# Moving ScalarE's rounding of weight chunks to the end of a step, and VectorE's rests from three chunks ahead to two

## The chip, the cores and the metric

The kernel runs on one core of one Trainium2 chip. Its time is the device time of one execution in microseconds (us). The core has a matrix engine (TensorE, PE in the rows), a vector engine (VectorE, DVE), a scalar engine (ScalarE, ACT), GpSimd (POOL) and a queue engine (SyncE, SP). Each engine works through its own program in order, and semaphores tie the five programs together. SP, POOL and ACT also issue DMA transfers between HBM and the on-chip memory.

## The reference

One inference step of one layer of a hybrid decoder, in float32. The 512 prompt positions and the 8 decode sequences (one new token each) go through the same weights, so the kernel handles 520 columns at once. What matters here, cut short:

```python
xn = rms_norm(x, norm1_g)
proj = xn @ w_in                    # D_MODEL 2048 -> pool 512, conv 3*512, q/k/v 3*1024, 8 forget logits
y_pool, y_conv = causal_pool_mix(...), h_b * causal_dwconv(h_c * h_x, prev_conv, conv_w)
q, k = rms_norm(q, q_norm_g), rms_norm(k, k_norm_g)     # 8 heads of 128
y_att = attn_fn(q, k, v, logf)      # prompt: causal, 512 x 512 per head
                                    # decode: 8 sequences, each over 4096 cached positions (32 pages of 128)
mix = concat([rms_norm(y_pool), rms_norm(y_conv), rms_norm(y_att)])
x = x + mix @ w_o
a, gate = split(rms_norm(x, norm2_g) @ w_up)            # 2048 -> 2 * 5632
x = x + (silu(causal_dwconv(a) + b) * gate) @ w_down    # 5632 -> 2048
```

The cached keys and values of the decode sequences are 256 pages each, and a page is 128 positions by 1024 numbers (512 KB).

## The kernel before

**Products in three parts.** A float32 product is made of three products of rounded numbers: a number is a rounded head plus a rest (`xh` and `xl` for the activations, `wh` and `wl` or `wlr` for the weights), and PE adds head times head, head times rest and rest times head. ScalarE makes the head of the weights (a Copy from the raw weights `wraw` to `wh`, in `head`), VectorE the rest (`wraw` minus `wh`, in `tile_rest` in the first part of the program, to `wlr`).

**Tiles, chunks and steps.** The input projection has 40 tiles of 128 output columns. A tile's weights are two *chunks* of 8 blocks of 128 x 128, so chunks 2t and 2t+1 belong to tile t, and there are `CHUNKS` = 80. The program of every engine is written as a loop over steps s. In PE's step s (2 to 79) stands `half_tile(s // 2, s % 2)`: the even step does the first 260 of tile s/2's columns, the odd one the other 260. So PE needs chunk 2t at the start of step 2t and chunk 2t+1 in the middle of step 2t. `half_tile` waits for `w_lo`, which counts the rests. The chunks are released (`w_used`) in the odd step, at its middle and at its end. `wh` has four slots, so the head of chunk c may be made once chunk c-4 is released. `wlr` has room for eight chunks.

**Raw weights.** `wraw` has two slots of 2 MB, each with four chunks. SP issues the load for chunks 4n to 4n+3 at the end of its step 4n-5, behind that step's key pages, and waits there until PE has finished its own step 4n-5 (line 683; `w_used`).

**What ScalarE does in a step.** In an odd step s it makes the head of chunk s+3, moves PE's accumulator of the half tile away (`keep_half`, with the 8 decode columns into `projS`), and makes the head of chunk s+4. In an even step it only moves the accumulator. After these come the stages of the pool mixer and of the prompt's attention heads (`pool_out`, `prompt_head`), and after all of it, where a sequence's value sum is complete, the move of that sum to `osb` (the `V_LAST` part).

**What VectorE does in a step.** Softmax bookkeeping of the decode sequences, stages of the prompt heads, then one page of keys times the query (`key_page`, line 1857: eight instruction pairs, one for each head), then `tile_rest(s + 3)`, then mixer parts, then the step's other two or three key pages. Key pages come through a ring of four buffers. SP issues the load of a page when VectorE has used the page four before it. All key pages (SP) and raw weights (SP) stand in one queue.

**Value pages.** PE multiplies them inside `half_tile` (two at a time), and POOL loads them into a second ring of four.

After step 79 come the mixers' norms, the output projection with the remaining value pages, and the feed-forward part, which is the longer half of the run.

Of the kernel before, what the change touches and what calls it, by code (L numbers as in the profile page):

```python
# [49 lines left out]
CHUNKS = 80  # L50
# [98 lines left out]
def hybrid_layer_kernel(nc, a, o):  # L149
    ctx = ExitStack()  # L150
    with ctx:
# [271 lines left out]
        def square_place(n):  # L423
            return stg[:, 0, 0:SEQ] if n < 14 else sq_late
# [842 lines left out]
        def _(act):  # L1267
            seq = Count(act_seq)

            def copy(out, in_):  # L1270
                return act.activation(out, in_, ACT.Copy)  # L1271
# [62 lines left out]
            def raw_chunk(c, down):  # L1334

                raw, q = wraw[:, (c // 4) % 2, :], c % 4
                if down:
                    return raw.rearrange("p (k n) -> p k n", k=FG)[:, :, q * 256:(q + 1) * 256]
                m, half = divmod(q, 2)
                return raw.rearrange("p (k n) -> p k n", k=KT)[:, half * 8:half * 8 + 8, m * P:(m + 1) * P]  # L1340

            def blocks(buf, c, down):
                return buf[:, c % 4, :].rearrange("p (k n) -> p k n", k=FG if down else 8)

            def head(g, c, down=False):

                if c % 4 == 0:
                    n = g // 4 + c // 4
                    late = 0 if n <= R_F else (n % 2) + 1
                    act.wait_ge(w_loaded[n % 2], 16 * (n // 2 + 1 + late))  # L1350
                act.wait_ge(w_used, g + (c + 1))
                copy(blocks(wh, c, down), raw_chunk(c, down)).then_inc(w_hi, 1)
# [39 lines left out]
            def keep_half(t, b):  # L1392

                place = tile_place(t)
                if b == 0:
                    place_free(t)
                    act.wait_ge(half_full, t + 1)
                    copy(place[:, 0:HALF], ps[:, 0, 0:HALF]).then_inc(acc_free[0], 1)
                    return
                act.wait_ge(w_used, 4 + 2 * t + 2)  # L1400
                copy(place[:, HALF:SEQ], ps[:, 1, 0:SEQ - HALF])
                copy(projS[:, TILES[t]:TILES[t] + 1, :], ps[:, 1:2, SEQ - HALF:HALF]).then_inc(acc_free[1], 1)
                act.wait_ge(acc_free[1], t + 2)
                act.sem_inc(tile_kept, 1)
# [24 lines left out]
            def mix_square(n, y):  # L1429
                act.wait_ge(x_sum, n)  # L1430
                act.activation(square_place(n), y, ACT.Square).then_inc(x_sq, 1)

            def mix_rstd(n, bank, size, place):

                act.wait_ge(x_tot, n)
                act.activation(place, ps[:, bank, :], ACT.Ln, bias=epsc[:, :], scale=1.0 / size).then_inc(x_log, 1)
                act.wait_ge(x_log, n)
                act.activation(place, place, ACT.Exp, scale=-0.5).then_inc(x_rb, 1)
# [82 lines left out]
            for s in range(SLOTS):  # L1521
# [11 lines left out]
                if s < CHUNKS and s % 2 == 0:  # L1533
                    keep_half(s // 2, 0)
                if s < CHUNKS and s % 2:
                    head(0, s + 3)
                    keep_half(s // 2, 1)
                    head(0, s + 4)
                if s == 8:
                    act.wait_ge(p_tr, 1)  # L1540
                    copy(stT, ps[:, 2, 0:480].rearrange("p (g b) -> p g b", g=POOL_G)).then_inc(p_stT, 1)
# [31 lines left out]
                if s == CHUNKS:  # L1573
                    mix_rstd(2, 2, 1024, msum[2])
                    for g in (2, 3):
                        act.wait_ge(v_done, g + 1)
                        mix_square(12 + g, ymix[:, 4 + g, 0:SEQ])
                if s == CHUNKS + 1:
                    mix_rstd(3, 5, 512, msum[1])
                    act.wait_ge(r_full, 2)  # L1580
                    copy(rows_s[64:64 + 2 * CONV_T, :], ps[64:64 + 2 * CONV_T, 3, 0:P]).then_inc(r_copied, 1)
                    copy(rows_s[32:32 + CONV_T * DEC, :], ps[32:32 + CONV_T * DEC, 3, P:2 * P]).then_inc(r_copied, 1)
# [99 lines left out]
        def _(dve):  # L1682
            seq = Count(dve_seq)

            def tt(out, in0, in1, op):
                return dve.tensor_tensor(out, in0, in1, op)  # L1686
# [64 lines left out]
            def raw_chunk(c, down):  # L1751
                raw, q = wraw[:, (c // 4) % 2, :], c % 4
                if down:
                    return raw.rearrange("p (k n) -> p k n", k=FG)[:, :, q * 256:(q + 1) * 256]
                m, half = divmod(q, 2)
                return raw.rearrange("p (k n) -> p k n", k=KT)[:, half * 8:half * 8 + 8, m * P:(m + 1) * P]
# [4 lines left out]
            def tile_rest(c):  # L1761

                dve.wait_ge(w_hi, c + 1)
                m, half = divmod(c % 4, 2)
                kept = wlr[:, (c // 4) % 2, :].rearrange("p (k n) -> p k n", k=KT)[:, half * 8:half * 8 + 8, m * P:(m + 1) * P]
                tt(kept, raw_chunk(c, False), blocks(wh, c, False).bitcast(F32), ALU.subtract).then_inc(w_lo, 1)
# [328 lines left out]
            for s in range(SLOTS):  # L2095
                softmax(s)
                if s == 6:
                    page_sums()
                if s == 8:
                    page_biases()  # L2100
                if s == 14:
                    value_lanes()
                if s == 9:
                    pool_rows()
                if s in (OWN_Q, OWN_Q + 5):
                    own_q((s - OWN_Q) // 5)
                kp = [divmod(n, PAGES) for n in KEYS.get(s, [])]
                at_head = head_stages(s)
                for h, stage in at_head:
                    prompt_head(h, stage)  # L2110
                if s in (OWN_K, OWN_K + 4):
                    sample_keys((s - OWN_K) // 4)
                if kp:
                    key_page(*kp[0])
                if s + 3 >= 4 and s + 3 < CHUNKS:
                    tile_rest(s + 3)
                if pool_slot(s) is not None:
                    pool_part(pool_slot(s))
                if s == POOL0 + 2:
                    dve.wait_ge(e_kept, 4)  # L2120
                    step(dve, seq, dve.memset(sums_pool, 0.0))
                if pool_slot(s - 2) is not None:
                    mix_sum(pool_slot(s - 2))
                for g in range(CONV_T):
                    if g < 2 and s == CONV_AT[g] + 2:
                        mix_sum(4 + g)
                    if s == CONV_AT[g]:
                        conv_part(g)
                if s == 28:
                    dve.wait_ge(d_loaded, 16)  # L2130
                    dve.tensor_scalar(crow, crow, -1.0, None, ALU.mult).then_inc(h_cm, 1)
                    dve.wait_ge(y_stored, 96)
                    dve.memset(msum[2], 0.0)
                if s == CHUNKS - 1:
                    mix_sum(13)
                if s == CHUNKS:
                    mix_sum(14)
                    mix_sum(15)
                if s == CHUNKS + 1:
                    dve.wait_ge(h_O, HEADS)  # L2140
                    dve.wait_ge(h_stored[1], 16 * HEADS)
                    dve.wait_ge(y_stored, 16 * 14)
                    for c in range(4):
                        weight_rest(0, CHUNKS + c)
                    dve.wait_ge(r_stored, 112)
                    sample_squares(0, 8)
                if s == CHUNKS + 2:
                    for t in range(0, 8, 2):
                        mix_pair(t)
                if s == CHUNKS + 3:  # L2150
                    for t in range(8, 16, 2):
                        mix_pair(t)
                if s == OUT0 + 1:
                    sample_sums(0, 2, Y_TOT)
                    sample_scale(0, 2, Y_RS)
                if s == OUT0 + 2:
                    step(dve, seq, dve.memset(sumsq[1], 0.0))
                if s >= OUT0:
                    c = s - OUT0
                    weight_rest(0, CHUNKS + c + 4)  # L2160
                    if c % 2 and c >= 3:
                        out_sum(c // 2 - 1)
                    if c % 2:
                        out_tile(c // 2)
                if s == LAST + 2:
                    sample_mix()
                    sample_squares(8, 16)
                if s == LAST + 3:
                    sample_sums(2, 3, YA_TOT)
                if s == LAST + 4:  # L2170
                    sample_scale(2, 3, YA_RS)
                for n in kp[1:]:
                    key_page(*n)
# [125 lines left out]
```

## Time and profile before

| | |
|---|---|
| median of 3 runs | 2797.38 us (2797.11 to 2801.74) |
| the profiled execution | 2798.29 us, span of the profile 2796.3 us |
| PE busy over the span | 94% |
| the stretch of steps 2 to 79 | about 89 to 905 us |
| PE busy in that stretch | 725.19 of 816 us |
| DMA engines busy in that stretch | 0.93 |

Times in rows are microseconds from the start of the span. A row of the timeline has the start, the length, the engine, the line of the kernel, the operation and its tiles. In brackets stands how long the engine had been idle before it, and who released it. Busy time of PE is modelled for pipelined matmuls, so the gaps in front of its matmuls say more than its share.

### The profile page before, as it was taken

The page shows a single profiled execution, that of the slowest core. Times are in us where ns is not written, and L with a number is a line of the kernel's source. Part 1 is how long each engine was busy: PE and PEld are TensorE (multiplying, and loading weights), DVE is VectorE, ACT ScalarE, POOL GpSimd, SP SyncE. Part 2 cuts the span into 40 slices and gives each one's busy share as a digit, 9 for nine tenths or more (in the row PEclk, how much of TensorE's full clock was granted, in tenths as well). Part 3 has the DMA queues.
Part 4 walks back from the last instruction along what each step waited for, and adds up shares of the span by engine and source line. Part 5 has one row for each costly group of instructions (what it writes and reads, how often), then busy time and mean ns, then how long its engine had stood idle before and what let it go on. Part 6 is the DMA issues. An engine that isn't in the chain of part 4 may idle for free.

```text
span 2796.3 us, 50751 instructions
## 1 busy us (share of the span) xinstructions
PE 2617.2 (94%) x19729; PEld 2342.8 (84%) x19729; DVE 1425.7 (51%) x5631; ACT 735.1 (26%) x1029; POOL 160.9 (6%) x326
## 2 busy tenths in 40 slices
PE   6788789999988799889999999999999999999998
PEld 3676667777776356569999999999999999999998
DVE  5698768767867622244434343434343434343433
ACT  5222123333332311132222222222222222222221
POOL 0100111111111122100000000000000000000000
PEclk8888889999989799979999999999999999999999
DMA  8778999999999897652222222222222222222221
GB/s 297 242 243 299 335 334 364 360 359 359 335 328 363 323 314 265 218 186 84 93 96 91 91 91 91 91 91 91 91 91 91 91 91 91 91 91 91 91 91 65
DMA packets 272292, 524.55 MB, mean 188 GB/s; under 512 B 16148, under 2 KB 181693, under 8 KB 270740
## 3 DMA queue, kind: packets, MB, share of 16 engines
q1 hardware_dynamic: 218717, 365.71, 38.0%
q0 software_dynamic: 39760, 142.46, 13.8%
q10 hardware_dynamic: 13575, 13.14, 1.4%
q8 instruction: 155, 2.54, 0.4%
q14 instruction: 85, 0.70, 0.1%
HBM read 501.84 MB, written 17.76 MB: 186 GB/s over the span
## 4 chain that ended last, share of the span: by engine, by line
PE 70%; DMA 13%; DVE 11%; issue 3%; SPq 2%; ACT 1%; POOL 0%; DVEq 0%; POOLq 0%; ACTq 0%
PE ps L749 69%; DMA t_r<-in_cache_k 9%; DVE t_r L1857 8%; DMA t_r<-in_cache_v 2%; DMA t_wraw<-in_w_in 1%; SPq L630 1%; PE ps L752 1%; DVE t_stg L1742 0%; DVE t_wlr L1686 0%; DVE t_S L1857 0%; DVE t_auxL L1686 0%; DVE t_work L1686 0%; DVE t_xl L1686 0%; SPq L683 0%; ACT t_wh L1271 0%
## 5 line engine op out<-in xcount | busy, mean ns | idle before, releaser
L749 PE MATMUL ps<-t_xh,t_wh 128*128 128x260 f32 (+1 forms) x4352 | 1080.3, 299 | 33.4 <-DVE t_wlr L1686 19.6
L749 PE MATMUL ps<-t_xl,t_wh 128*128 128x260 f32 (+1 forms) x4352 | 1053.1, 294 | 0.0
L749 PEld LDWEIGHTS ps<-t_xh,t_wh 128*128 128x128 f32 x4352 | 745.8, 193 | 166.7 <-issue 119.2
L1686 DVE TENSOR_TENSOR t_wl<-t_wraw,t_wh 128x1024 fp32r<-128x1024 f32 x296 | 362.3, 1225 | 843.7 <-ACT t_wh L1271 843.7
L1271 ACT ACTIVATE t_wh<-t_wraw 128x1024 fp32r<-128x1024 f32 x376 | 398.5, 1060 | 1479.9 <-PE ps L749 1369.8
L749 PEld LDWEIGHTS ps<-t_xl,t_wh 128*128 128x128 f32 x4352 | 744.7, 193 | 10.7 <-issue 1.4
L749 PE MATMUL ps<-t_xh,t_wl 128*128 128x260 f32 (+1 forms) x3072 | 677.1, 294 | 0.0
L1857 DVE CUSTOM_DVE_ANT_0 t_r<-t_r,t_work 128x128 f32<-128x128 f32 x2048 | 455.4, 286 | 175.3 <-DMA t_r<-in_cache_k 159.0
L749 PEld LDWEIGHTS ps<-t_xh,t_wl 128*128 128x128 f32 x3072 | 487.5, 189 | 11.8
L749 PE MATMUL ps<-t_xh,t_wlr 128*128 128x260 f32 x1280 | 376.1, 294 | 0.0
L749 PE MATMUL ps<-t_hh,t_wh 128*128 128x260 f32 x1408 | 282.8, 282 | 3.4 <-issue 3.4
L749 PE MATMUL ps<-t_hl,t_wh 128*128 128x260 f32 x1408 | 284.4, 283 | 0.0
L749 PE MATMUL ps<-t_hh,t_wl 128*128 128x260 f32 x1408 | 284.2, 283 | 0.0
L749 PEld LDWEIGHTS ps<-t_xh,t_wlr 128*128 128x128 f32 x1280 | 257.3, 201 | 0.0
L1686 DVE TENSOR_TENSOR t_r<-ps,t_r 128x520 f32<-128x520 f32 (+1 forms) x184 | 128.5, 699 | 226.8 <-PE ps L749 226.8
L749 PEld LDWEIGHTS ps<-t_hh,t_wh 128*128 128x128 f32 x1408 | 217.1, 189 | 4.5 <-issue 3.7
L749 PEld LDWEIGHTS ps<-t_hh,t_wl 128*128 128x128 f32 x1408 | 216.6, 189 | 0.0
L749 PEld LDWEIGHTS ps<-t_hl,t_wh 128*128 128x128 f32 x1408 | 216.4, 188 | 0.0
L749 PE MATMUL ps<-t_r,t_work 128*8 128x512 f32 x1040 | 163.5, 629 | 33.4 <-DMA t_r<-in_cache_v 23.7
L552 POOL DMA_DIRECT2D t_r<-in_cache_v x256 | 135.7, 530 | 847.4 <-PE ps L749 820.5
L1857 DVE DVE_READ_ACCUMULATOR2_ANT t_S<- 128x1 f32 x2048 | 167.0, 82 | 0.1
L1686 DVE TENSOR_TENSOR t_wlr<-t_wraw,t_wh 128x1024 fp32r<-128x1024 f32 x80 | 97.4, 1219 | 12.1 <-ACT t_wh L1271 12.1
(305 smaller groups left out, 1243.0 us busy)
## 6 DMA issues: line engine op xcount, KB each, us to landing
t_r<-in_cache_k SPq DMA_DIRECT2D x256, 512.0 KB, 6.7
t_r<-in_cache_v POOLq DMA_DIRECT2D x256, 512.0 KB, 7.0
t_wraw<-in_w_up SPq DMA_DIRECT2D x44, 2048.0 KB, 8.0
t_wraw<-in_w_down SPq DMA_DIRECT2D x22, 2048.0 KB, 7.8
t_wraw<-in_w_in SPq DMA_DIRECT2D x21, 2048.0 KB, 16.2
t_wraw<-in_w_o SPq DMA_DIRECT2D x11, 2048.0 KB, 14.0
scr_x<-t_r POOLq DMA_DIRECT2D x1, 4160.0 KB, 20.0
t_work<-in_x_prompt SPq DMA_DIRECT2D x4, 1024.0 KB, 6.6
```

The costliest lines, as they stand in the source:

```text
L552: pool.dma_start(vring[:, n % RING, :], v_pages[bass.ds(g, 1), :, :].rearrange("a p n -> (a p) n")).then_inc(v_loaded[n % RING], 16)
L630: return sp.value_load(ptr[0:1, bass.ds(n, 1)], min_val=0, max_val=N_POOL - 1)
L749: return pe.matmul(out, lhsT, rhs, start=start, stop=stop)
L752: return pe.transpose(out, in_, ident[0:n, 0:n])
L1271: return act.activation(out, in_, ACT.Copy)
L1686: return dve.tensor_tensor(out, in0, in1, op)
L1857: last = dve.tensor_tensor_reduce(out=kring[:, p % RING, h * HD:(h + 1) * HD], in0=kring[:, p % RING, h * HD:(h + 1) * HD], in1=qcur[r % 2 ...
```

## The change

ScalarE's two heads of an odd step are taken out of their places around the accumulator's move. In their stead each step from 1 to 80 makes one head, of chunk s+3, behind the accumulator's move, the pool mixer's parts and the stages of the prompt heads. VectorE's step makes the rest of chunk s+2 instead of s+3, at the same place in the step.

```diff
@@ ScalarE, step s @@
                 if s < CHUNKS and s % 2:
-                    head(0, s + 3)
                     keep_half(s // 2, 1)
-                    head(0, s + 4)
...
                         mix_square(12 + g, ymix[:, 4 + g, 0:SEQ])
+                if 1 <= s <= CHUNKS:
+                    head(0, s + 3)
                 if s == CHUNKS + 1:
@@ VectorE, step s @@
                     key_page(*kp[0])
-                if s + 3 >= 4 and s + 3 < CHUNKS:
-                    tile_rest(s + 3)
+                if 4 <= s + 2 < CHUNKS:
+                    tile_rest(s + 2)
```

The same heads and rests are made, in the same numbers. The programs of PE, SP and POOL are unchanged, row for row.

ScalarE before, from step 28's end to step 30: the head of chunk 32, the two moves of step 29's accumulator (`t_work<-ps`, `t_projS<-ps`), the head of chunk 33, head 0's logarithms and exponential, then the move of the first sequence's value sum (`t_work<-ps 128x512`) and step 30's accumulator.

```order
L1271 ACTIVATE t_wh<-t_wraw 128x1024
L1271 ACTIVATE t_work<-ps 128x252
L1271 ACTIVATE t_projS<-ps 128x8
L1271 ACTIVATE t_wh<-t_wraw 128x1024
L1469 ACT_TABLE_LOAD
L1469 ACTIVATE t_auxL<-ps,t_epsc 128x512
L1470 ACTIVATE t_auxL<-ps,t_epsc 128x512
L1473 ACT_TABLE_LOAD
L1473 ACTIVATE t_auxL<-t_auxL 128x1024
L1271 ACTIVATE t_work<-ps 128x512
L1271 ACTIVATE t_auxL<-ps 128x260
```

And now, the same place: the accumulator's moves of step 29 first, then the head stage, then the head of chunk 32, then the value sum, then step 30's accumulator and behind it the head of chunk 33.

```order
L1271 ACTIVATE t_work<-ps 128x252
L1271 ACTIVATE t_projS<-ps 128x8
L1469 ACT_TABLE_LOAD
L1469 ACTIVATE t_auxL<-ps,t_epsc 128x512
L1470 ACTIVATE t_auxL<-ps,t_epsc 128x512
L1473 ACT_TABLE_LOAD
L1473 ACTIVATE t_auxL<-t_auxL 128x1024
L1271 ACTIVATE t_wh<-t_wraw 128x1024
L1271 ACTIVATE t_work<-ps 128x512
L1271 ACTIVATE t_auxL<-ps 128x260
L1271 ACTIVATE t_wh<-t_wraw 128x1024
```

Chunk 32's head moved from before the accumulator to behind the exponential, and chunk 33's from step 29 to step 30.

VectorE, the first place of difference: its step 1, between the forget gate's instructions and the first key page.

```order
 L1809 SCALAR_TENSOR_TENSOR t_work<-t_work 8x520
 L1810 SCALAR_TENSOR_TENSOR t_work<-t_work 8x512
-L1686 TENSOR_TENSOR t_wlr<-t_wraw,t_wh 128x8x128
 L1857 ISA t_r,t_S<-t_r,t_work 128x128
 L1857 ISA t_S 128x1
```

One rest is gone there and one appears at the end, in step 77. At the 75 places between, the rows read alike, and each now makes the rest of the chunk before the one that it made.

## Rows read from the trace of the kernel before

**Rows 1.** Windows: stretch, its us; busy PE, PEld, DVE, ACT, POOL; PEclk, DMA, GB/s.

```profile
89.00:905.00 816.00, 725.19 (x5079) 596.02 (x5079) 624.89 (x4358) 241.00 (x435) 92.78 (x175) 0.91 0.93 333
400.00:905.00 505.00, 473.61 (x3374) 378.19 (x3372) 375.76 (x2662) 170.75 (x317) 65.31 (x123) 0.95 0.97 354
1254.00:2796.00 1542.00, 1530.48 (x12715) 1528.37 (x12714) 616.57 (x911) 362.61 (x411) 5.08 (x10) 1.00 0.27 90
```

**Rows 2.** Waits from 89 to 905 us: total, times, longest.

```profile
DVE t_r L1857 <- DMA t_r<-in_cache_k: 159.0, 40, 12.2
ACT t_wh L1271 <- DMA t_wraw<-in_w_in: 80.2, 10, 16.5
...
PE ps L749 <- DVE t_auxL L1958: 21.3, 4, 7.5
PE ps L749 <- DVE t_wlr L1686: 19.6, 4, 10.2
...
DVE t_wlr L1686 <- ACT t_wh L1271: 3.8, 2, 2.9
...
PE ps L749 <- ACT t_auxL L1271: 3.4, 1, 3.4
```

**Rows 3.** Timeline of SP: raw weights (L683) and key pages (L634).

```profile
263.20 0.39 SPq L683 DMA_DIRECT2D t_wraw<-in_w_in  x1
265.44 46.67 SPq L634 DMA_DIRECT2D t_r<-in_cache_k  x14
...
397.56 0.39 SPq L683 DMA_DIRECT2D t_wraw<-in_w_in  x1
...
857.16 0.39 SPq L683 DMA_DIRECT2D t_wraw<-in_w_o  x1
```

**Rows 4.** Timeline of VectorE: first key page behind raw weights, and rests.

```profile
283.56 0.29 DVE L1857 CUSTOM_DVE_ANT_0 t_r<-t_r,t_work 128x128 f32<-128x128 f32 x1 [9.29 <-DMA t_r<-in_cache_k]
...
285.27 1.22 DVE L1686 TENSOR_TENSOR t_wlr<-t_wraw,t_wh 128x1024 fp32r<-128x1024 f32 x1
...
291.97 1.22 DVE L1686 TENSOR_TENSOR t_wlr<-t_wraw,t_wh 128x1024 fp32r<-128x1024 f32 x1
...
413.43 0.29 DVE L1857 CUSTOM_DVE_ANT_0 t_r<-t_r,t_work 128x128 f32<-128x128 f32 x1 [11.19 <-DMA t_r<-in_cache_k]
...
425.11 1.21 DVE L1686 TENSOR_TENSOR t_wlr<-t_wraw,t_wh 128x1024 fp32r<-128x1024 f32 x1
```

**Rows 5.** Timeline of PE: its gaps, and the passage from step 29 to 30.

```profile
127.27 0.58 PE L749 MATMUL ps<-t_xh,t_wh 128*128 128x260 f32 x1 [10.15 <-DVE t_wlr L1686]
286.55 0.39 PE L749 MATMUL ps<-t_xh,t_wh 128*128 128x260 f32 x1 [4.45 <-DVE t_wlr L1686]
332.90 0.59 PE L749 MATMUL ps<-t_xh,t_wh 128*128 128x260 f32 x1 [3.94 <-DVE t_wlr L1686]
362.41 1.88 PE L749 MATMUL ps<-t_auxL,t_ones 128*128 128x512 f32 x4
374.15 1.04 PE L749 MATMUL ps<-t_r,t_work 128*8 128x512 f32 x4 [7.70 <-issue]
```

**Rows 6.** Timeline of ScalarE: moves of accumulators and heads of chunks.

```profile
299.75 0.36 ACT L1271 ACTIVATE t_work<-ps 128x252 f32<-128x252 f32 x1
...
366.05 1.06 ACT L1271 ACTIVATE t_wh<-t_wraw 128x1024 fp32r<-128x1024 f32 x1 [9.13 <-DMA t_wraw<-in_w_in]
367.01 0.36 ACT L1271 ACTIVATE t_work<-ps 128x252 f32<-128x252 f32 x1
...
373.47 0.58 ACT L1271 ACTIVATE t_work<-ps 128x512 f32<-128x512 f32 x1
...
432.95 0.38 ACT L1271 ACTIVATE t_work<-ps 128x252 f32<-128x252 f32 x1 [2.97 <-PE ps L749]
```

**Rows 7.** The window behind the gap that ends at 374.15.

```profile
374.00:379.00 5.00, 4.85 (x22) 3.18 (x23) 4.76 (x46) 0.05 (x1) 1.06 (x2) 0.50 0.55 167
```

**Rows 8.** Part 6 of the page: load, KB each, median us from issue to landing.

```profile
t_wraw<-in_w_in SPq DMA_DIRECT2D x21, 2048.0 KB, 16.2
```

## The prediction

> **What bounds the kernel now.** I read the windows first, since the change acts only while the input projection runs, about 89 to 905 us. From 1254 us on PE is busy without a break at the full granted clock (1.00) [rows 1]: that half can't move, and what the change costs or gives before it comes out one for one at the end. In the stretch itself three things are close to full at once: PE 725.19 of 816 us, the DMA engines 0.93, VectorE 624.89 of 816. From 400 us on PE is at 473.61 of 505 and the DMA engines at 0.97 [rows 1]. So nobody has much room, and what counts is which wait joins the three.
>
> The table of waits says which. VectorE waits for key pages (159.0 us in 40 waits) and hardly for ScalarE's heads (3.8). PE waits for VectorE's rests four times, 19.6 us in all, and for an accumulator's move once, 3.4 [rows 2]. ScalarE waits 80.2 us for raw weights [rows 2], in every fourth step ahead of the accumulator's move.
>
> The pattern is one of four steps, since SP loads raw weights every fourth step. Take the group that begins when SP issues raw weights at 263.20, at the end of PE's step 19, and the key page of step 20 behind them at 265.44 [rows 3]. That page is used at 283.56, after VectorE idled 9.29 us for it [rows 4]. The 2048 KB of raw weights go ahead of it in the queue, and take 16.2 us to land in the median [rows 8]. Right behind the page stands the rest of chunk 23 (285.27, done 286.49), and PE, which stood in the middle of step 22, starts again at 286.55 after 4.45 us of idleness [rows 5]. The waits at 127.27 and 332.90 are the same wait, for chunks 7 and 27. So already the lead of three chunks runs out once every four steps, for the odd chunk whose rest stands behind the late key page.
>
> **The change part by part.**
>
> *Rests one step later.* No rest is added: 76 of 1.22 us stay in the stretch. But the rest of a chunk now stands where that of the next one stood. For chunk 23 this is the place at 291.97, done at 293.19 [rows 4], 6.7 us later than 286.49, at a point where PE waits already. I put every chunk's new place (the next rest's end before) against the time at which PE reached it. Of the 75 chunks 4 to 78, 35 would come late, the worst of each group of four from chunk 4 to 67 by 13, 4, 3, 0, 8, 10, 9, 8, 3, 5, 8, 4, 8, 3, 1 and 1 us, and from step 68 on none.
>
> *What a late rest costs.* If VectorE went on undisturbed, PE would fall behind once, by the worst lateness, 8 to 13 us, and then have its rests in time. It would win back what it now idles for VectorE. But VectorE isn't undisturbed: SP issues the raw weights only when PE has finished the fourth step, and the key pages queue behind them. That closes a loop: end of PE's step 4m+3, raw weights and key page, VectorE's step 4m+4, in step 4m+5 the rest of chunk 4m+7, PE from the middle of step 4m+6 to the end of 4m+7. Its length from the first group: 20.4 us (263.20 to 283.56) plus 9.6 (to 293.19) plus 13.2 (286.55 to the move at 299.75 [rows 6]) = 43.2 us, where that group took 36.6 (263.20 to 299.75). In the group from 397.56: 15.9 to 413.43, 12.9 to 426.32, 13.2 = 42.0, where it took 35.4 (to 432.95). So the loop adds 6.6 us to each of these two. The 14 groups between 263.20 and 857.16 [rows 3] take 42.4 us on average: the long ones (47 to 50 us) hide the loop, the short ones don't. Lining up all 19 groups by this sum, each with its own three parts, nine are lengthened: by 5.3, 5.8, 0.9, 7.9, 4.7, 3.7, 2.7, 7.7 and 0.8, 39 us in all. That is the upper bound.
>
> *What comes off it.* First, the page behind the raw weights comes sooner when PE, not VectorE, is last to release them, since the earlier key pages have then landed: 15.9 us in the group from 397.56, against 20.4 and an average of 17.7. I take 2 us off in each of 8 groups, 16 us. Second, PE's gaps that VectorE or ScalarE cause go when PE is later: 21.3 us in four waits for the pool mixer (they swallow the 5.3 of the first group), 7.70 at 374.15. Of these I take 14. 
>
> *Heads behind the stages.* ScalarE is busy 241.00 of 816 us, and a head is 1.06 us. Chunk 23's head now comes after step 20's accumulator instead of after step 19's. VectorE takes it in step 21, behind 291: 20 us later. So heads cost nothing; the cover is VectorE's lag of over a step, and if that went, each head would hold VectorE up by a few us. The gain is that the move and the head stages no longer stand behind the wait for raw weights. It shows once on the path: at 366.05 the head of chunk 32 ended a wait of 9.13 us, behind it came step 29's accumulator at 367.01, the head stage, and at 373.47 the value sum's move, for which PE waited 7.70 us, to 374.15 [rows 5, 6]. Now the stage, 4.9 us of work in front of that move, begins behind step 29's end (362.41, where PE sums the head's squares [rows 5]) and passes during that wait; a head of 1.06 stands behind it, and the sum moves at about 370, 3 to 4 us sooner. This is in the 14 above.
>
> Sum: 39 - 16 - 14 + 4 = +13 us. The profiled execution took 2798.29, within 1 us of the median 2797.38. **Forecast 2810 us.**
>
> *A rule against the trace.* The trace has 20.4 us for a key page behind raw weights, while value pages share the engines. The Trainium skill (DMA: Bandwidth & Descriptors, Queues, rings and completion order) says that each DMA engine goes round-robin over the queues that have work. By it a stalled PE, which frees no value pages, would hand its share to SP's queue. No run here separates the two queues. What it would make of the time is rival B.
>
> **The rivals.**
>
> A, *all is passed on*: the loop binds as computed and nothing is absorbed, +39, 2836 us. For it: the DMA share of 0.97 and PE's 473.61 of 505. Against: VectorE-caused gaps exist and would close. Chance 0.14.
>
> B, *the lateness is absorbed*: while PE stalls, no value pages are asked for, and the key page lands sooner. The raw weights (2048 KB) and one page (512 KB) are 2.6 MB; at 354 GB/s [rows 1] that is 7.4 us instead of 17.7, so the loop would shrink to about 33 us, under any group. Then PE only lags once and takes it back in its other gaps: 2797 to 2802 us. Against: PE's stall comes after the page has landed, not before. Chance 0.13. By the Trainium skill's rule this would be the likelier one.
>
> C, *faster*: the loop's lateness is absorbed as in B and ScalarE's freed moves decide. The gap of 7.70 us goes with its slow clock of 5 us (2.5), and the 3.4 for an accumulator with it, up to 12 us with what the earlier head stages save at the pool mixer: 2786 us. It decides if PE waits for rests less than 20 us in all, as now. For it: 80.2 us of waits for raw weights stand before ScalarE's moves. Against: PE waited for a move of an accumulator just once. Chance 0.15.
>
> **How the numbers follow.** The forecast, slower by 6 to 28 us, has 0.58; A 0.14, B 0.13, C 0.15. A measurement of this kernel can't tell a difference under 0.2% (5.6 us) from none. Slower by more: 0.58 + 0.14 = 0.72; within it B, 0.13; faster C, 0.15. The range from 2789 to 2832 leaves out the outer part of A and of C, about 0.07 each. The forecast's own range is 2803 to 2826.
>
> **What would show it.** In the changed profile PE's waits for `t_wlr` rise from 19.6 us to 50 to 90, ten or more of them, at the start and in the middle of steps 4m+2. VectorE's waits for key pages stay near 159 or rise. SP's raw issues wait more for PE. The last accumulator's move (step 79) comes 8 to 25 us later than before. The wait of 7.70 at 374.15 shrinks, and PE's waits for the pool mixer's `t_auxL` L1958 fall under 21.3. ScalarE's waits for raw weights shift behind the moves; VectorE's for heads stay under 15. I would be wrong if PE's waits for rests stay near 20, or if they rise and step 79 still ends at its old time.

## The result, and the profile after

| | before | after |
|---|---|---|
| median | 2796.86 us, 6 runs (2793.4 to 2801.74) | 2820.47 us, 6 runs (2811.73 to 2828.52) |
| profiled execution | 2798.29 us, span 2796.3 us | 2819.47 us, span 2817.5 us |
| ratio | | 1.0074, 95% interval 1.006 to 1.0089 |

The change makes the kernel slower by 0.74%, which is 20.7 us, where +13 us was forecast. (This goes by the ratio. The two medians of the table lie 23.6 us apart, the two profiled executions 21.2.) The windows of the kernel after have the same columns as [rows 1]:

```profile
89.00:914.70 825.70, 724.93 (x5062) 599.04 (x5062) 621.19 (x4323) 231.62 (x431) 90.66 (x172) 0.91 0.91 325
400.00:928.00 528.00, 481.55 (x3384) 384.13 (x3382) 383.90 (x2680) 170.33 (x321) 65.74 (x124) 0.94 0.95 343
1275.00:2817.00 1542.00, 1530.62 (x12732) 1528.22 (x12731) 617.24 (x912) 363.99 (x412) 5.08 (x10) 1.00 0.27 90
```

The last row is the late half, 1542 us as before, with 1530.62 us of PE against 1530.48. So the whole difference arises in the input projection. The accumulator's last move (step 79) starts at 914.7 us, before at 894.0: 20.7 us later. From 400 us on the DMA engines fell from 0.97 to 0.95 and from 354 to 343 GB/s [rows 1]: the same bytes took longer.

The first row ends at that last move. For the kernel before the same row, cut at its own last move, is:

```profile
89.00:894.00 805.00, 719.78 (x5061) 595.19 (x5061) 616.93 (x4295) 235.91 (x430) 90.26 (x171) 0.91 0.92 332
```

PE was busy 5.15 us longer for the same matmuls. The other 15.4 us of the 20.7 are waits. What PE waited for in that stretch, after the change (total, times, longest):

```profile
PE ps L749 <- DVE t_wlr L1686: 68.5, 23, 7.2
PE ps L749 <- DVE t_auxL L1958: 9.6, 3, 4.6
...
PE ps L749 <- issue: 2.6, 2, 2.3
```

All of PE's waits add up to 103.6 us in ten kinds, before to 88.2 in thirteen. Waits for rests grew from 19.6 us in 4 times [rows 2] to 68.5 in 23, by 48.9. All others together shrank from 68.6 to 35.1, by 33.5: the mixer's from 21.3 to 9.6, those of the kind "issue" (the 7.70 us at 374.15 among them [rows 5]) from 13.1 to 2.6. What ScalarE and VectorE waited for in the kernel after:

```profile
DVE t_r L1857 <- DMA t_r<-in_cache_k: 165.0, 35, 13.1
...
ACT t_wh L1271 <- DMA t_wraw<-in_w_in: 2.6, 2, 2.4
```

ScalarE's wait for raw weights has shrunk from 80.2 us to 2.6, and VectorE's 3.8 us for heads [rows 2] have no row any more. SP's program shows the other side of PE's lateness. Its wait for PE ahead of the raw weights, before:

```profile
SPq L683 <- PE ps L749: 28.4, 7, 9.4
```

and after:

```profile
SPq L683 <- PE ps L749: 61.3, 14, 11.2
```

So in 14 of the 20 loads PE is now last to release SP, before in 7. One turn of the loop, of the group that begins at 399.14. SP issues raw weights, and the next key page behind them:

```profile
399.14 0.39 SPq L683 DMA_DIRECT2D t_wraw<-in_w_in  x1
401.94 1.55 SPq L634 DMA_DIRECT2D t_r<-in_cache_k  x1
```

VectorE idles for the page, makes the rest behind it, and in the next step the other one:

```profile
415.07 0.29 DVE L1857 CUSTOM_DVE_ANT_0 t_r<-t_r,t_work 128x128 f32<-128x128 f32 x1 [12.09 <-DMA t_r<-in_cache_k]
...
416.78 1.22 DVE L1686 TENSOR_TENSOR t_wlr<-t_wraw,t_wh 128x1024 fp32r<-128x1024 f32 x1
...
426.64 1.22 DVE L1686 TENSOR_TENSOR t_wlr<-t_wraw,t_wh 128x1024 fp32r<-128x1024 f32 x1
```

PE starts right behind that rest (done at 427.86):

```profile
427.92 0.59 PE L749 MATMUL ps<-t_xh,t_wh 128*128 128x260 f32 x1 [5.50 <-DVE t_wlr L1686]
```

and the accumulator of step 35 is moved at 441.69, where SP's next load of raw weights is issued, behind a wait for PE. The three parts are 15.9, 12.8 and 13.8 us (399.14 to 415.07, to 427.86, and 427.92 to 441.69), 42.5 in all. The prediction had 15.9, 12.9 and 13.2 for this group. Its other worked group did not come out: from the end of step 19 to that of step 23 it forecast 43.2 us, and the trace has 38.3 (265.9 to 304.2), against 36.5 before. The key page came 17.4 us after the load instead of 20.4, and PE waited once, for the rest right behind that page (5.8 us, to 286.1), and not for the one a step later.

**Where the 20.7 us arise.** The stretch can be cut at the end of step 31, which is 397.8 us before and 399.4 after. The windows before:

```profile
89.00:397.80 308.80, 249.38 (x1697) 216.43 (x1698) 247.00 (x1680) 68.98 (x116) 27.47 (x52) 0.85 0.85 299
397.80:894.00 496.20, 470.39 (x3365) 378.76 (x3363) 369.93 (x2616) 166.93 (x315) 62.79 (x119) 0.95 0.97 353
```

and after:

```profile
89.00:399.40 310.40, 248.65 (x1698) 215.31 (x1699) 249.34 (x1696) 67.38 (x117) 27.96 (x53) 0.88 0.84 297
399.40:914.70 515.30, 476.29 (x3366) 383.73 (x3364) 371.85 (x2627) 164.24 (x315) 62.70 (x119) 0.94 0.95 342
```

| | first part, before | after | second part, before | after |
|---|---|---|---|---|
| length | 308.8 | 310.4 | 496.2 | 515.3 |
| PE's waits for rests | 18.5 | 47.9 | 1.0 | 20.6 |
| PE's other waits | 40.8 | 16.7 | 24.4 | 18.0 |

So 47.9 of the 68.5 us of waits for rests stand in the first part, and they cost 1.6 us there: PE's other waits fell by 24.1. The second part has 20.6 of them and 19.1 of the 20.7 us. In five of its twelve groups of four steps (those behind the ends of steps 31, 39, 43, 51 and 75) SP waited for PE at the raw weights, VectorE for the key page behind them and PE for a rest. These five are 25.2 us longer than before, the other seven 6.1 us shorter in sum. The trace of VectorE's half of the change alone (below) has the same split: 51.8 of its 75.5 us of waits for rests in the first part, which took 312.3 us, and 510.6 us for the second. These are single executions, and six of the kernel after spread over 17 us, so the split is good to some us only.

### The profile page after: what moved, and what is told of

Same layout as the page of the kernel before. It is cut to its first block, busy times and chain, and to the rows that moved or that the text cites. A ratio compares the mean times of both kernels' runs of the same rounds, so it can differ in the third digit from the quotient of the medians.

```text
span 2817.5 us, 50751 instructions
## 1 busy us (share of the span) xinstructions
PE 2621.4 (93%) x19729; PEld 2345.9 (83%) x19729; DVE 1426.2 (51%) x5631; ACT 731.1 (26%) x1029; POOL 160.7 (6%) x326
## 3 DMA queue, kind: packets, MB, share of 16 engines
q0 software_dynamic: 39760, 142.46, 13.8%
## 4 chain that ended last, share of the span: by engine, by line
PE 74%; DMA 11%; DVE 9%; issue 3%; SPq 2%; ACT 1%; POOL 0%; POOLq 0%; DVEq 0%; ACTq 0%
PE ps L749 73%; DMA t_r<-in_cache_k 8%; DVE t_r L1857 6%; DMA t_r<-in_cache_v 3%; DMA t_wraw<-in_w_in 1%; SPq L630 1%; PE ps L752 1%; DVE t_wlr L1686 1%; DVE t_stg L1742 0%; SPq L634 0%; DVE t_auxL L1686 0%; DVE t_xl L1686 0%; SPq L649 0%; DVE t_S L1857 0%; DVE t_work L1686 0%
## 5 line engine op out<-in xcount | busy, mean ns | idle before, releaser
L749 PE MATMUL ps<-t_xh,t_wh 128*128 128x260 f32 (+1 forms) x4352 | 1084.4, 300 | 82.8 <-DVE t_wlr L1686 68.5
L749 PEld LDWEIGHTS ps<-t_xl,t_wh 128*128 128x128 f32 x4352 | 747.4, 194 | 10.6 <-issue 1.2
L1857 DVE DVE_READ_ACCUMULATOR2_ANT t_S<- 128x1 f32 x2048 | 174.4, 85 | 0.1
L1271 ACT ACTIVATE t_work<-ps 128x512 f32<-128x512 f32 (+7 forms) x81 | 38.2, 486 | 287.6 <-PE ps L749 263.1
## 6 DMA issues: line engine op xcount, KB each, us to landing
t_wraw<-in_w_in SPq DMA_DIRECT2D x21, 2048.0 KB, 15.9
```

Source lines behind the costliest of these rows:

```text
L749: return pe.matmul(out, lhsT, rhs, start=start, stop=stop)
L1857: last = dve.tensor_tensor_reduce(out=kring[:, p % RING, h * HD:(h + 1) * HD], in0=kring[:, p % RING, h * HD:(h + 1) * HD], in1=qcur[r % 2 ...
```

## The experiments

Three theories about the +20.7 us stood before the first runs. **L**: a late rest makes PE late, PE makes SP's raw weights late, and with them the key page and the next rests. **H**: ScalarE's new places cost. **O**: PE lags once and the rest is absorbed. Each kernel ran beside the kernel before on one chip; the ratios are to that one. The median of before beside them was 2800.9, 2800.4 and 2801.6 us in the three batches.

### ScalarE's half of the change alone

```diff
-                    head(0, s + 3)
                     keep_half(s // 2, 1)
-                    head(0, s + 4)
...
+                if 1 <= s <= CHUNKS:
+                    head(0, s + 3)
```

> ScalarE as in the changed kernel (heads behind the stages), VectorE as before (rest of chunk s+3). Theory L (the late rests cost the time, through the loop of raw weights and key pages): the rests keep their old places, so the time is near the kernel before, 2795 to 2804 us, with PE's waits for t_wlr at 15 to 30 us. VectorE should now wait for heads for the first time, 10 to 40 us in all in t_wlr <- t_wh, mostly near steps 31, 59, 67, 70 and 71, where it is less than a step behind PE. Rival H (ScalarE's heads or moves in their new places cost the time): 2812 to 2822 us.

Measured: 2803.91 us, ratio 1.0013 (1.0002 to 1.0024). Its waits:

```profile
DVE t_r L1857 <- DMA t_r<-in_cache_k: 116.2, 31, 12.2
DVE t_wlr L1686 <- ACT t_wh L1271: 55.2, 13, 9.1
PE ps L749 <- DVE t_wlr L1686: 22.0, 5, 10.2
```

With the rests left at three chunks ahead, VectorE does run into the later heads: 55.2 us, where before it was 3.8 [rows 2]. It costs little: VectorE waits 42.8 us less for key pages (159.0 to 116.2). H is out as the cause: 0.13% of 0.74%.

### VectorE's half alone

```diff
-                if s + 3 >= 4 and s + 3 < CHUNKS:
-                    tile_rest(s + 3)
+                if 4 <= s + 2 < CHUNKS:
+                    tile_rest(s + 2)
```

> ScalarE as before, VectorE as in the changed kernel (rest of chunk s+2). Theory L: all of the loss is here, 2813 to 2824 us, PE's waits for t_wlr 60 to 75 us; a few us more than the changed kernel if the earlier moves of accumulators and value sums give something (the wait of 7.70 us at step 30 would be there again). Rival H: 2794 to 2801 us.

Measured: 2822.66 us, ratio 1.0074 (1.0046 to 1.0101), the whole loss of the change.

```profile
PE ps L749 <- DVE t_wlr L1686: 75.5, 26, 9.6
```

SP waited 57.7 us for PE in 13 loads, about as in the kernel after. ScalarE's half neither adds nor takes away beside it.

### The change, with rests ahead of the step's first key page

```diff
-                if kp:
-                    key_page(*kp[0])
                 if 4 <= s + 2 < CHUNKS:
                     tile_rest(s + 2)
+                if kp:
+                    key_page(*kp[0])
```

> The changed kernel, but in each step the rest of chunk s+2 stands ahead of the step's first key page, not behind it. The chunk that stood behind the page that comes after the raw weights (4m+6) is then free of it, and the rest of chunk 4m+7 comes about 3 us sooner after that page (one page of 1.9 us and one rest of 1.2 us less in front of it). Theory L: the loop is 3 us shorter in each group, so more than half of the loss is gone: 2800 to 2810 us, PE's waits for t_wlr at 20 to 40 us. Rival O (PE merely lags once behind VectorE and no loop is closed): the one lateness shrinks by 3 us, 2812 to 2819 us.

Measured: 2807.48 us, ratio 1.0021 (1.0008 to 1.0035). Some 15 us are back (a ratio of 1.0021 instead of 1.0074), by moving the same rests over one page's wait.

```profile
PE ps L749 <- DVE t_wlr L1686: 55.7, 14, 11.8
```

PE's waits for rests stayed above the 20 to 40 us expected: fewer (14 for 23), each longer. So their sum is a poor measure of the loss. Of the 55.7 us, 38.0 stand before the end of step 31.

### The kernel before, with the rest ahead of the page in every fourth step

The three large waits for rests in the kernel before [rows 5] were for the chunk whose rest stands behind the late page. This moves that one rest only.

```diff
+                if s % 4 == 0 and s and s + 3 < CHUNKS:
+                    tile_rest(s + 3)
                 if kp:
                     key_page(*kp[0])
-                if s + 3 >= 4 and s + 3 < CHUNKS:
+                if s % 4 and s + 3 >= 4 and s + 3 < CHUNKS:
                     tile_rest(s + 3)
```

> The kernel before, but in steps 4, 8, 12 and so on the rest of chunk s+3 stands ahead of the step's first key page, the one that comes behind the raw weights. Its head is there already. Theory L: the four waits of PE for these rests (19.6 us) go, and what is behind them is the next bound: 2782 to 2792 us. Rival O, or the view that PE and the transfers together bound the stretch: PE gains and gives it back by waiting elsewhere, 2794 to 2799 us.

Measured: 2790.06 us, ratio 0.9955 (0.9939 to 0.9972).

```profile
PE ps L749 <- DVE t_wlr L1686: 2.4, 2, 1.9
```

The 19.6 us of waits for rests [rows 2] became 2.4, and the last move came at 883.4 instead of 894.0. The same place that the change worsens can be bettered, and then the kernel is faster. Of the 10.6 us only 3.7 are there at the end of step 31, where 18.5 of the 19.6 us had stood; how the other 6.9 come about isn't shown.

### Variants of that: all rests ahead, and heads behind the stages

All rests ahead of the page, in the kernel before:

> The kernel before with the rest of chunk s+3 ahead of the first key page in every step. In three of four steps PE did not wait for the rest, so there is nothing to gain beyond the 0.45% of e6; where VectorE is close behind PE the rest waits for its head and the page behind it with it. 2787 to 2796 us.

Measured: 2791.29 us, ratio 0.9964 (0.9939 to 0.999). Not to be told from the fourth-step variant: the other rests show no gain.

The fourth-step variant, with both heads of the steps 4m+1 made behind the stages and behind the value sum's move:

> As e6, and in steps 5, 9, 13 and so on, where ScalarE waits for raw weights, both heads go behind the accumulator's move, the head stages and the value sum's move. If the wait of PE for the value sum at step 30 (7.70 us before) is due to the heads in front of it, it goes: 2782 to 2789 us. If VectorE's rests then wait for heads as in e1 (55.2 us), 2790 to 2797.

Measured: 2792.46 us, ratio 0.9969 (0.9952 to 0.9987). Nothing is gained in all by ScalarE's freed moves, though the 7.70 us gap [rows 5] was the case for them and has gone in this trace. Step 31 ended at 387.5 us, where the fourth-step variant has 394.1, but the last move came at 890.1 instead of 883.4. VectorE waited 14.0 us for heads.

### One chunk ahead

The kernel after with `tile_rest(s + 1)`. L says that the loop then binds in every group.

> The changed kernel with VectorE's rest one chunk later still (chunk s+1 in step s). A dose: theory L closes a loop of raw weights and key page (17 us), one more VectorE step (about 20 us from the page to the rest of chunk 4m+7 instead of 10) and PE's 14 us: 51 us for four steps against 42.6 in the changed kernel, about 9 us in each of 18 groups: 2900 to 2990 us, with SP's raw loads waiting for PE in nearly every group. Rival O (PE lags once, by one VectorE step more, no loop): 2825 to 2840 us.

Measured: two runs, 3011.98 us at a mean granted clock of 0.927 and 3216.22 us at 0.773, beside 2800.4 us at 0.955 to 0.962 for the kernel before. The profiled one is the slower, with a clock of 0.85 also where PE is busy without a break, so only direction and pattern are read from it.

```profile
PE ps L749 <- DVE t_wlr L1686: 208.9, 28, 14.8
...
DVE t_r L1857 <- DMA t_r<-in_cache_k: 178.7, 25, 16.8
```

```profile
SPq L683 <- PE ps L749: 247.9, 19, 20.4
```

SP waited for PE in 19 loads, nearly every group. L says so, but a PE slowed by its clock would give the same. The faster run lost 212 us, over the 100 to 190 us expected. In the profiled one PE's waits for rests grew by 140 us over those of the kernel after; how the loss divides between loop and clock stays open, and this experiment carries little.

### The raw weights behind the next step's key pages

The loop has another edge. SP's program holds the key pages of step 4m+4 behind a load that waits for PE. Here, on top of the version with rests ahead of the page, the same load with the same wait stands one step's key pages later:

```diff
-                if s % 4 == 3 and s < CHUNKS:
-                    n = (s - 3) // 4 + 2
+                if s % 4 == 0 and 4 <= s <= CHUNKS:
+                    n = (s - 4) // 4 + 2
                     sp.wait_ge(w_used, 4 + 4 * (n - 1))
```

> As e4 (changed kernel, rest ahead of the step's first page), and SP issues the raw weights one step's key pages later (behind the pages of step 4m+4 instead of 4m+3), with the same wait for PE. Then no rest of chunks 4m+6 and 4m+7 stands behind a key page that stands behind raw weights. Theory L: PE's waits for t_wlr fall from 55.7 us in e4 to under 20, and the time to 2790 to 2800 us, though the rests are still one step later than before. Rival: what counts is that the rests are a step later, wherever the raw weights stand, or the raw weights now come too late for their own heads: 2803 us or more, with PE's waits moved to chunks 4m+8.

Measured: 2760.8 us, ratio 0.9866 (0.9843 to 0.9889), 1.3% faster than the kernel before, and well beyond what was expected of it.

```profile
89.00:865.00 776.00, 704.76 (x5079) 577.70 (x5079) 633.25 (x4366) 238.19 (x438) 94.47 (x177) 0.95 0.96 351
400.00:865.00 465.00, 447.93 (x3294) 356.88 (x3286) 374.19 (x2611) 165.57 (x308) 64.50 (x121) 0.99 1.00 374
```

The DMA engines are full (1.00, 374 GB/s) from 400 us on, and the granted clock is 0.99. SP's program around the load of the group that began at 399.14 above:

```profile
378.47 6.59 SPq L634 DMA_DIRECT2D t_r<-in_cache_k  x4
387.13 0.39 SPq L683 DMA_DIRECT2D t_wraw<-in_w_in  x1
395.01 6.38 SPq L634 DMA_DIRECT2D t_r<-in_cache_k  x4
```

The key pages of step 32 are issued ahead of the load now; the first of them was used at 393.05, 6 us behind PE's end of step 31 (387.4), where before it took 15.9.

### The same edit on three kernels

Which part of the 1.3% is the order in SP's program (Q), and which needs the early rests (R)? On the kernel before:

> The kernel before, and the raw weights are loaded behind the key pages of the next step instead of ahead of them. Theory Q (what the last but one batch gained, 2760.8 us, came from the order in which SyncE's program issues: the key pages of every fourth step stood behind a load that waits for the tensor engine): most of the gain is here already, 2765 to 2785 us, and SyncE's wait for the tensor engine at the raw load falls from 28.4 us to under 10. Rival R (the gain needs the rests early as well, since a raw load one step later comes late for rests that stand behind a key page): 2790 to 2815 us, and the tensor engine waits over 35 us for rests.

Measured: 2775.73 us, ratio 0.9913 (0.9896 to 0.9929). On the kernel after:

> The kernel after, and the raw weights behind the key pages of the next step. By theory Q: 2770 to 2790 us; the loop by which late rests make the raw weights late is cut where it held up the key pages, and the tensor engine waits under 50 us for rests (68.5 us in the kernel after). By rival R: 2810 to 2835 us, with over 70 us.

Measured: 2775.01 us, ratio 0.9913 (0.9894 to 0.9932). This is the run on which the cause rests most. With SP's load out of the way of the key pages, the change costs nothing: 2775.0 against 2775.7 us, where without the edit it costs 0.74%. Both windows, of before with the edit:

```profile
400.00:883.00 483.00, 462.28 (x3354) 369.40 (x3346) 379.00 (x2668) 169.24 (x317) 65.96 (x124) 0.97 0.99 368
```

and of after with the edit, with PE's and SP's waits:

```profile
400.00:881.00 481.00, 460.30 (x3334) 368.07 (x3332) 376.42 (x2649) 167.69 (x317) 64.66 (x123) 0.97 0.99 367
```

```profile
PE ps L749 <- DVE t_wlr L1686: 58.1, 14, 11.6
```

```profile
SPq L683 <- PE ps L749: 5.4, 2, 4.6
```

PE still waits 58.1 us for rests here. But all its waits to the last move are 79.5 us, against 76.5 in the kernel before with the edit, of which 1.5 for rests. The lateness takes the place of other waits, as O says. The place matters again: 50.2 of the 58.1 us stand before the end of step 31, where such waits cost almost nothing without the edit too. Behind it the edit leaves 7.9 of the 20.6 us, and both kernels take the same time there, 478.0 and 477.3 us, with the DMA engines at 0.99. The expectation that the waits for rests would fall under 50 us was wrong.

Two things move with this edit: SP's wait for PE, and the 2 MB transfer that stands ahead of the key page in the queue. No run moves one without the other. So it is shown that the load's place costs the 0.74%, but not how it divides between the two. For the gain on the kernel before (0.87%) the trace speaks for both. Of the 21.6 us by which its last move came sooner, 9.9 are in the six groups behind a load at which SP had waited for PE, and 13.8 in the other thirteen (step 3 ended 2.1 us later).

On the kernel with the fourth step's rest ahead:

> The kernel before with rests ahead of the page in every fourth step (2790.06 us), and the raw weights behind the key pages of the next step. If the two gains add up (-0.45% and theory Q's part): 2750 to 2765 us. If ScalarE's and VectorE's new places of the change carry part of the 2760.8 us: 2765 to 2785 us.

Measured: 2777.57 us, ratio 0.9916 (0.9899 to 0.9932). The gain of the early rest (0.45%) is not there a second time. On the kernel after it is: the 2760.8 us kernel is the one of 2775.0 with rests ahead of the page, 14 us faster. What differs are the change's own edits, and that the rests stand ahead of the page in every step there and in every fourth here. With the heads in their old places ScalarE waited 190.0 us for raw weights ahead of its moves, in the 2760.8 us kernel 55.7, behind them. That this makes the 14 us is a guess; it was not run by itself.

The load another step later, on the 2760.8 us kernel:

> The 2760.8 us kernel with the raw weights two steps later instead of one. By theory Q there is nothing left to gain in the issue order (SyncE waited 5.9 us there), and the margin of the rounding and the rests shrinks by one step of about 10 us: 2775 to 2830 us, and ScalarE waits over 20 us for raw weights. Rival: the load is hidden anyway and the key pages gain once more: 2745 to 2762 us.

Measured: 2786.78 us, ratio 0.9955 (0.9938 to 0.9971).

```profile
ACT t_wh L1271 <- DMA t_wraw<-in_w_in: 202.3, 17, 17.9
...
DVE t_wlr L1686 <- ACT t_wh L1271: 91.5, 18, 8.3
DVE t_r L1857 <- DMA t_r<-in_cache_k: 34.7, 37, 6.8
```

VectorE's waits for key pages are down to 34.7 us (106.8 in the 2760.8 us kernel), and the raw weights are late instead. Of the three distances run on this kernel (2807.48, 2760.8 and 2786.78 us) one step is the best.

Letting SP wait for VectorE's rests alone, not for PE, would take SP's wait for PE away altogether. It wasn't tried: `wlr` lies in the memory of `wraw` (the rests are written over the raw weights), so the load must wait for PE's use of them.

## Why the prediction was right, and where its sum was off

**What bounds the stretch: held.** The late half didn't move (1542 us), and what was lost before it came out one for one.

**The loop: held, in fewer places than forecast.** The signs came as named: waits for rests of 50 to 90 us in ten or more (68.5 in 23), SP waiting for PE in 14 loads, and the last move 20.7 us later (8 to 25 predicted). Of the two worked groups the one at 399.14 matches within 1 us, the one at 265.65 is 4.9 us shorter than forecast. That the late rests are the cause is shown by VectorE's half alone (the whole loss), and that they cost by way of SP's load by the edit in SP's program (no loss left). SP's wait and the transfer's place in the queue were not separated.

**Heads at no cost: held,** and the cover named was the right one. In the change the rests moved back with the heads. Where they don't, VectorE waits 55.2 us for heads, and even that costs only 0.13%. A small miss: ScalarE's waits for raw weights did not shift behind the moves, they went (80.2 to 2.6 us).

**The sum: mis-sized, with errors that partly cancel.** It can be set against PE's time up to the last move:

| term | predicted | measured |
|---|---|---|
| lateness of rests, less sooner key pages | 39 - 16 = +23 | waits for rests, +48.9 |
| PE's other gaps | -14 | -33.5 |
| slower clock behind stalls | +4 | +5.15 of busy time |
| sum | +13 | +20.6 |

The rows are not quite alike: the first predicted term is time added to groups, the measured one is waits. It helps to take the two parts of the stretch apart. In the first, 29.4 us more of waits for rests met 24.1 us less of others: the lateness was absorbed, as rival B and theory O have it. The prediction had only 14 us for that in the whole stretch; it counted the mixer's waits and the one at 374.15, and PE's lag closed small ones of many kinds as well (those for `t_mx`, `t_maxall` and `t_diag` have no row after the change or a smaller one). In the second part 19.6 us more of waits for rests met only 6.4 us less of others, and PE was busy 5.9 us longer at a clock of 0.94 for 0.95.

The term that failed is the first, +39 called an upper bound and 16 taken off it. The 39 put each group's three parts of the kernel before in a line, so it held VectorE's timetable fixed outside the loop. It had nine groups lengthened. The trace has the whole chain (SP, VectorE and PE each waiting) in seven, two of them in the first part, and those seven are 27.0 us longer. Of all 19 groups of four steps 13 are longer, by 40.1 us, and six shorter, by 19.1, which the sum had no term for. How the nine come about isn't shown either: they add up to 39.5, and 6.6 us, the sum of each worked group, is not among them.

The key page behind the raw weights did come sooner, by 1.1 us in the mean over the 14 loads from step 19 to 71 (16.9 us for 18.0), 15 us in all. The prediction had it as 2 us in each of eight groups that bind. In the 13 where SP now waits over 1 us for PE it was 1.0 (17.1 for 18.1), 13 us in all. So the 16 came near in sum with the size twice too large and the number of groups too small.

That +13 fell near enough to 20.7 is in part luck, then. The mechanism is the one forecast, but an overstated upper bound, a deduction for pages that came near by two errors, and other gaps at less than half their size stand behind the number.

**A, all passed on:** 33.5 us of other waits did go, so it wasn't all. In the second part, where the DMA engines are at 0.97 in the kernel before, it came near to that: 19.1 us longer with 19.6 us more of waits for rests. **B, the lateness is absorbed:** this is what the first part shows (1.6 us for 29.4), though not by B's means: a page 1.1 us sooner is far from the 10 us (7.4 for 17.7) that B needed. The Trainium skill (DMA: Bandwidth & Descriptors, Queues, rings and completion order) says that each DMA engine goes round-robin over the queues that have work, and by that rule B was the likelier. The page that came only 1.1 us sooner speaks against B, not against the rule, since no run here separates the queues. Over the whole stretch B's end state came true only in the kernel with SP's edit. **C, faster:** the 7.70 us gap went as foretold, and the variant that moves heads behind the stages on a kernel without late rests gained nothing by it (0.9969 against 0.9955).

What the prediction did not see is that the kernel before paid for the same load's place. It named SP's wait as what passes lateness on, and didn't price it, or the page behind the 2 MB, where nothing is late: moving the load gained 0.87% of the kernel before.

## What to carry to other kernels

Where a queue engine's program holds a load that waits for a consumer, read what is issued behind it. In this kernel those loads were late by that wait and by the load's own transfer, and they fed the engine that feeds the consumer, so a lateness could go round. Before costing a later stage at "lateness times so many", ask by which edge the lateness comes back, and whether something else has room for it. Here waits for rests took the place of other waits in the first part of the stretch, where PE had 40.8 us of those and the DMA engines were at 0.85. The 19.6 us more of them in the second, at 24.4 us and 0.97, went with 19.1 us more time. That the room makes the difference is read from these rows and was not tested by itself.

A wait's total says little of its price: 55.7 us of it stood beside +0.21%, 58.1 beside -0.87%, 68.5 beside +0.74%. Cut it by place before using it.

## What the runs showed of the hardware

From 400 us on, while the input projection ran, the DMA engines reached a share of 1.00 at 374 GB/s in the fastest kernel, against 0.97 at 354 in the kernel before. So what looked like a full resource in [rows 1] still carried 5 to 6% more. PE's granted clock in the same stretch was 0.99 in the fastest kernel, 0.95 in the kernel before and 0.94 after the change, and PE waited 12.2, 25.4 and 38.6 us behind the end of step 31. But a total of waits does not give the clock: in the part up to step 31 PE waited 59.3 us before and 64.6 after, and the clock was 0.85 and 0.88.
